# One run for attention, output projection and query projection, with the sample group's attention steps inside the projection's tiles

## The reference, cut to what matters

```
s    = q k^T * 64**-0.5 - slope_h * |i - j|       # two maps per head, 4 heads, blocks of 128 queries
attn = softmax(s[0]) - lam * softmax(s[1])
o_da = head_rms(attn @ v) * (1 - lam_init)
o_hg = head_rms(o_fwd + o_bwd) * silu(hg)         # o_fwd, o_bwd, silu(hg) come from earlier stages
x    = x + concat(o_hg, o_da) @ w_out
q    = rms_norm(x, g_ca) @ w_cq                   # queries of the cross attention that follows
```

## Time and profile before

| | |
|---|---|
| median of 3 runs | 2218.47 us (2218.03 to 2220.35) |
| the profiled execution, its own time | 2217.62 us |
| its span, first to last instruction | 2216.1 us |
| PE / DVE / ACT busy over the span | 89% / 61% / 53% |
| attention stage, first load to barrier | about 726.6 to 944.4 us |
| output projection | about 944.4 to 1108.7 us |
| query projection | about 1108.7 to 1234.6 us |

### The profile page before, as it was taken

One profiled execution on the slowest core, in us unless ns is written; L12 is line 12 of the kernel. 1 busy time (PEld: TensorE's weight loads), 2 busy tenths in 40 slices (PEclk: granted clock), 3 DMA queues, 4 the chain that ended last, 5 costly groups with the idle time before them and its releaser, 6 DMA issues. The chain is left out here.

```text
span 2216.1 us, 31313 instructions
## 1 busy us (share of the span) xinstructions
PE 1978.8 (89%) x11108; PEld 1640.8 (74%) x11108; DVE 1362.0 (61%) x1801; ACT 1180.8 (53%) x1767; POOL 265.2 (12%) x304
## 2 busy tenths in 40 slices
PE   6999999979999699559889499986999999999990
PEld 5888888858888376448778388875888888888870
DVE  4222231019997588646411035546999999999986
ACT  4334432118776588713222133222888888888873
POOL 0000000020000011100000000000122232332210
PEclk9999999989999799779989699996999999999995
DMA  5223422136552400244233423234999999999987
GB/s 171 97 93 135 151 98 105 46 105 188 177 174 91 176 15 15 74 147 169 77 120 115 138 90 111 72 148 148 337 384 379 383 379 383 375 379 391 385 315 318
DMA packets 162984, 423.98 MB, mean 191 GB/s; under 512 B 18880, under 2 KB 84544, under 8 KB 136768
## 3 DMA queue, kind: packets, MB, share of 16 engines
q1 hardware_dynamic: 137424, 342.37, 43.1%
q0 software_dynamic: 25456, 80.24, 9.4%
HBM read 354.92 MB, written 82.31 MB: 197 GB/s over the span
## 5 line engine op out<-in xcount | busy, mean ns | idle before, releaser
L113 PE MATMUL cross_ot_ps<-w_w_high,cross_o_high 128*128 128x512 f32 x544 | 220.7, 406 | 2.9 <-DVE cross_o_low L2140 2.4
L115 PE MATMUL cross_ot_ps<-w_w_high,cross_o_low 128*128 128x512 f32 x544 | 213.9, 393 | 0.0
L113 PE MATMUL front_acc<-in_high,front_w_high 128*128 128x512 f32 (+1 forms) x480 | 170.5, 355 | 0.0
L114 PE MATMUL front_acc<-in_low,front_w_high 128*128 128x512 f32 (+1 forms) x480 | 170.2, 354 | 0.0
L115 PE MATMUL front_acc<-in_high,front_w_low 128*128 128x512 f32 (+1 forms) x480 | 170.0, 354 | 0.0
L2107 DVE TENSOR_TENSOR cross_low_up<-cross_raw_up,w_w_high 128x2048 fp32r<-128x2048 f32 x68 | 152.8, 2289 | 12.1 <-ACT w_w_high L1918 12.1
L2107 DVE TENSOR_TENSOR cross_low_down<-cross_raw_down,w_w_low 128x2048 fp32r<-128x2048 f32 x68 | 152.7, 2287 | 1.7 <-ACT w_w_low L1918 1.6
L2107 DVE TENSOR_TENSOR w_w_low<-cross_raw_gate,w_w_high 128x2048 fp32r<-128x2048 f32 x68 | 152.2, 2279 | 0.0
L1918 ACT ACTIVATE w_w_high<-cross_raw_up 128x2048 fp32r<-128x2048 f32 x68 | 126.2, 1908 | 0.0
L1918 ACT ACTIVATE w_w_low<-cross_raw_down 128x2048 fp32r<-128x2048 f32 x68 | 126.1, 1906 | 0.0
L1918 ACT ACTIVATE w_w_high<-cross_raw_gate 128x2048 fp32r<-128x2048 f32 x68 | 126.0, 1902 | 0.0
(11 more groups left out here) (364 smaller groups left out, 4984.0 us busy)
## 6 DMA issues: line engine op xcount, KB each, us to landing
cross_raw_gate<-in_w_gate_dram SPq DMA_DIRECT2D x68, 1024.0 KB, 7.3
cross_raw_down<-in_w_down_dram SPq DMA_DIRECT2D x68, 1024.0 KB, 7.8
cross_raw_up<-in_w_up_dram SPq DMA_DIRECT2D x68, 1024.0 KB, 9.2
front_raw<-in_w_in_dram SPq DMA_DIRECT2D x32, 512.0 KB, 4.4
hgrn_raw<-in_w_ckv_dram SPq DMA_DIRECT2D x16, 512.0 KB, 6.4
cross_y_kept<-y_rows SPq DMA_DIRECT2D x16, 512.0 KB, 9.5
k_t<-front_staged POOLq DMA_DIRECT2D x8, 640.0 KB, 3.3
lf_t<-front_staged_lf POOLq DMA_DIRECT2D x8, 640.0 KB, 4.6
```

The costliest lines, as they stand in the source:

```text
L113: pe.matmul(out, lhs[0], rhs[0], start=first, stop=False)
L114: pe.matmul(out, lhs[0], rhs[1], start=False, stop=False)
L115: return pe.matmul(out, lhs[1], rhs[0], start=False, stop=last)
```

## The change

One function, `attend_mix_query`, takes the place of the three. There is one program block and so one barrier at its end. All orders are written out without loops.

Buffers of the later part are laid over those of the earlier part that are dead by then (query, keys and bias of the first three heads become `of`, `ob`, `silu`, `mixed` and the split of `mixed`; the normalised tokens go over the last head's bias, values, scores and probabilities). The eight PSUM banks are divided anew: `out_ps` has banks 0 and 1, the transposes of `mixed` one bank (2) instead of two, the sample scores banks 3 and 4, `xt_ps` banks 6 and 7; the query accumulators are banks 2 to 4 and 5 to 7.

The prompt's query, keys and values are loaded without the sample's tokens, which come in three loads of their own after them. The split of `w_out` moves from the last 8 steps to the prompt steps 2, 5, 8, ... 23. The first tiles' `sum_heads` and `gate` run in the prompt steps 25 to 30. The transposes of `mixed`, their split, the product and the residual are cut into halves of 512 columns with semaphores of their own. The 8 sample steps are cut up and placed at "points": point p = 2t + half is one half of tile t's product, and step s has its scores in the middle of product s + 2, transposes after product s + 3, output after product s + 4. The query projection starts right behind the last product. Its moving operand is `h_t`, which holds tokens in tiles (tile, high or low, k, 128), so that a 512-column operand is four runs of 128 columns.

```diff
-    steps = [(first, seq, h, t) for first, seq in ((0, SEQ_P), (SEQ_P, SEQ_S)) for h in range(HEADS) ...]
-    riders = {N - KC + r: r for r in range(KC)}
+    steps = [(h, t) for h in range(HEADS) for t in range(NT_P)]                 # N = 32
+    s_steps = [(h, t) for h in range(HEADS) for t in range(NT - NT_P)]          # NS = 8
+    riders = {2 + 3 * r: r for r in range(KC)}
+    first_point = 2
# GpSimd's queue
+                for t in range(NT):
+                    for p in (2 * t, 2 * t + 1):
+                        s = p - first_point - 2
+                        if 0 <= s < NS:
+                            store_sample(s)        # waits for s_o_done, s_head_norm(s)
+                    if t >= 1:
+                        store_x1(t - 1)
+                        if t + 1 < NT:
+                            load_x(t + 1)          # waits for the store of tile t - 1 to land
# VectorE
+                for n in range(-4, N):
+                    attention(n + 2); head_norm(n); find_least(n + 4)   # each where in range
+                    if n in riders: subtract_out(riders[n])
+                    if n == N - 7: sum_heads(0)
+                    if n == N - 6: gate(0)
+                    if n == N - 5: sum_heads(1)
+                    if n == N - 4: low_part(0, 0); gate(1)
+                    if n == N - 3: low_part(0, 1); sum_heads(2); low_part(1, 0); residual(0, 0)
+                    if n == N - 2: low_part(1, 1); gate(2); residual(0, 1)
+                for t in range(1, NT):
+                    sum_heads(t + 2); scale_next(t - 1); low_part(t + 1, 0); low_next(t - 2)
+                    for half in range(2):
+                        s = 2 * t + half - first_point
+                        s_find_least(s)
+                        residual(t, half)
+                        s_attention(s)
+                        if half == 0: low_part(t + 1, 1)
+                        s_head_norm(s - 2)
+                        if half == 0: gate(t + 2)
+                subtract_query(0); low_next(last_tile - 1); scale_next(last_tile); ...
# ScalarE, in a tile t
+                    find_next_rstd(t - 1); round_mixed(t + 1, 0); round_next(t - 2)
+                    for half in range(2):
+                        s_exps(s); s_copy_attention(s - 1); s_attention_rstd(s - 2)
+                        if half == 0: head_rstd(t + 2); round_mixed(t + 1, 1)
# TensorE
+                def s_transposes(s):
+                    pe.wait_ge(s_attn_done, s + 1)
+                    pe.wait_ge(s_attn_t_done, s)
+                    pe.wait_ge(s_score_read, min(s + 2, NS))
+                    ...
+                def product(t, half):                # waits m_low_done, x1_half_done or x1_done
+                    for k in range(KC):
+                        product3(...)
+                        if k == KC // 2 - 1: s_scores(s)
+                    s_transposes(s - 1); s_output(s - 2)
+                mixed_transposes(1, 0)               # after the scores, outputs, transposes of step N - 4
+                output(N - 2)
+                product(0, 0)
+                transposes(N - 1)
+                mixed_transposes(1, 1)
+                product(0, 1)
+                output(N - 1)
+                for t in range(1, NT):
+                    mixed_transposes(t + 1, 0); product(t, 0)
+                    mixed_transposes(t + 1, 1); product(t, 1)
+                    next_transposes(t - 1)
+                queries(0, 0)                        # waits q_low_done 1 and xt_low_done 4
+                next_transposes(last_tile)
+                queries(0, 1)
+                queries(0, 2)
+                for c in range(1, blocks):
+                    for group in range(3): queries(c, group)
# the caller
-            diff_attention(...); mix_out(...); project(...)
+            attend_mix_query(...)
```

More of the change, by code:

```diff
@@ L154, in rows_of @@
     return rows[ds(i * (2 * P) + u * P, P), :]
[L157 to L185, removed]
@@ L188, in project @@
[L188 to L297, removed]
@@ L1145, in _, with attend_mix_query @@
                 output(NT - 1, 1)
[L1148 removed]
+def attend_mix_query(nc, tag, dq_t, dk_t, dv_rows, g_da, lam, w_out, o_fwd, o_bwd, g_rows, mix, x_rows, g_hg, x1_out,
+                     g_next, w_cq, q_out, w_co, w_high, w_low, ident, eps):
     slopes = [2.0 ** (-8.0 * (h + 1) / HEADS) for h in range(HEADS)]
[L1154 to L1157, removed]
[L1158 to L1192 removed]
@@ new lines, in _ @@
+                load_heads(1)
+                load_attention(0)
+                load_attention(1)
+                for t in range(2, NT):
+                    load_heads(t)
+                    load_attention(t)
+                sp.wait_ge(mixed_done, NT)
+                load_query_weight(0)
+                load_query_weight(1)
+                sp.wait_ge(out_ready, 2 * NT)
+                load_co(0)
+                load_co(1)
+                for c in range(2, blocks):
+                    load_query_weight(c)
+                    load_co(c)
@@ new lines, in _ @@
+                for n in range(-4, N):
+                    if 0 <= n + 2 < N:
+                        attention(n + 2)
+                    if n >= 0:
+                        head_norm(n)
+                    if n + 4 < N:
+                        find_least(n + 4)
+                    if n in riders:
+                        subtract_out(riders[n])
+                    if n == N - 7:
+                        sum_heads(0)
+                    if n == N - 6:
+                        gate(0)
+                    if n == N - 5:
+                        sum_heads(1)
+                    if n == N - 4:
+                        low_part(0, 0)
+                        gate(1)
+                    if n == N - 3:
+                        low_part(0, 1)
+                        sum_heads(2)
+                        low_part(1, 0)
+                        residual(0, 0)
+                    if n == N - 2:
+                        low_part(1, 1)
+                        gate(2)
+                        residual(0, 1)
@@ L1269, in _ @@
+                subtract_query(0)
+                low_next(last_tile - 1)
+                scale_next(last_tile)
+                subtract_query(1)
+                low_next(last_tile)
+                for c in range(blocks):
+                    if c + 2 < blocks:
+                        subtract_query(c + 2)
+                    subtract_co(c)
             @block.scalar
@@ L1278, in exps @@
                 def exps(n):
[L1279 removed]
+                    u = n % 2
                     act.wait_ge(score_read, n + 1)
```

742 lines of the change are left out of this document (515 added, 227 removed).

## The result

The changed kernel takes **2193.85 us** (median of 4 runs, 2192.68 to 2196.01), the kernel before 2218.25 us beside it (2217.55 to 2220.35): ratio 0.989, 95% interval 0.9872 to 0.9907. That is 24.4 us faster. The forecast was 57.7 us, range 2146 to 2182: the sign is right, and more than half of the gain is missing; the time lies outside the range. The profiled execution is the one of 2192.68 us, span 2191.0; its mean granted clock is 0.953.

A forecast was written before the change was run, and what follows sets the result against it. PE was taken to bound products, query projection and prompt steps, with DVE and ACT nearly full in the latter; two seams held 95 us, PE needing 35.5. Terms summed to -57.7 us, giving 2160.8 us from a 2218.5 median, range 2146 to 2182.

The forecast's parts named there:

- The rows of `w_out`: Prompt steps: splitting eight `w_out` rows there costs ACT nothing and delays DVE 0.38 us each, +3.0 us, bounds 0 and 9.2.
- The block's end: Behind the query projection's last copy: nothing changes, since `q_t`'s store outlasts the last `w_co` row; 0 us.
- Ten tiles: Products with sample steps in them: 129.4 to 145.9 us, +16.5, bounds 139.4 and about 159.
- the loop of 18.3 us: Tiles 3 and 4: x arrives late through POOL's queue, 9.7 us plus 8.6 to the last head norm, setting the tile length.
- The first seam: Last prompt step's `find_least` to first product: 78.2 to 14.8 us, -63.4, as sample steps, barrier and fresh loads vanish.
- the second: Seam from last product to first query product: 17.0 to 1.9 us, -15.1, bounds 0.9 and 5.
- heads and gates: First tiles' `sum_heads` and `gate` in prompt steps: next `find_least` 1.4, then 2.1 us late, +3.5 us, bounds 0 and 4.4.
- The start: Before the first `find_least`: fewer tokens queued ahead of the small gain row, so DVE opens sooner, -2.7 us.
- rival (d): Query projection: split moving operands run at a lower rate, 1.1 us per cent, 2271 us at double; chance 0.04.
- (a): Tiles: PE alone sets them, x arrives in time and riders are free, 2147 us; chance 0.15.
- (b): Sample tiles: PE idles 2 to 4 us in tiles 3 to 5, falling to half clock each time, 2168 to 2184; chance 0.2.
- (c): Tiles: sample steps cost what they cost alone, some 4.5 us each, 36 in place of 16.5, 2180 us; chance 0.08.

The follow-up runs named there:

- e1: The changed kernel with DVE subtracting each row of `w_out` one step later in its queue: 2170.59 us.
- e7: The kernel of e1 with PE's first product placed ahead of the second tile's half transpose instead of behind it: 2169.09 us.
- e6: The kernel of e1 with GpSimd storing and loading x first in each tile turn, the two sample stores behind: 2165.27 us.
- e8: The changed kernel with the late subtraction, an added GpSimd drain after its last store of x, and x first in GpSimd's turn: 2160.07 us.
- e10: The kernel of e1 with an extra GpSimd drain behind 34 of its 68 DMAs, ahead of its loop over tiles: 2167.72 us.

## Why the prediction was wrong, and where it was right

**The rows of `w_out`: the failed step.** It was this sentence: ACT "is ahead of its consumer, so it costs nothing", and with it the +3.0 us, 0.38 a row, for DVE. The runs showed 27.9 us in its place, 3.5 a row. The work was sized nearly right: with the wait removed (e1) a row costs 0.42 to 0.45 us, although its 1.04 us of rounding don't fit into the 0.51 that ACT has spare in one step. What the sum left out is that DVE's subtraction needs ACT's rounding of the same step, and that ACT's place for it is at the end of a step that waits for PE's output. DVE reaches the subtraction 2.5 us before that. Moving a pair of operations on two engines adds an edge between their queues, and I priced the two operations and not the edge. It stood in a row that I had read: the subtraction in the earlier trace rows is preceded by 2.53 us of idle for that very rounding. I took its 1.23 us and dropped the bracket. Nor was that wait harmless where it stood. The view of that line, and PE's next transposes, in the kernel before:

```profile
  ACT w_w_high L179: 13.7, 8
913.97 0.44 PE L1333 MATMUL da_attn_ps<-kept_ident,da_prob 128*128 128x128 f32 x2 [2.58 <-DVE da_prob L1252]
```

All eight rows together held DVE for 13.7 us, the first one kept PE waiting 2.58 us behind it, and from one `find_least` to the next it took 5.63 us there (908.46 to 914.09) for 2.27 just before. The granted clock, 1.00 until then, fell about 1 us after that stop. So this very wait made the sample steps of before longer. The upper bound of 9.2 us (no slack at all) was too low because it bounded work only. Eight times the bracket, 8 x 2.53 = 20.2, would have been most of the missing term; the runs showed 24.3 us between the changed kernel and e1 in these steps (27.9 less 3.6), of which some 3 go with the two falls of the clock.

**The block's end: not seen.** "After the last copy nothing changes" looked at `q_t`'s store and the `w_co` row, which was true, and not at the barrier. One block in place of three collects 68 DMAs on GpSimd for one drain (5.6 us), where the query projection had 8 (0.7). The rows were in the trace of before, among the sequencers' instructions. The Trainium skill (VectorE: DVE Perf Modes, The DRAIN you can't avoid) describes, beside the pipeline flush, a boilerplate drain of about 12 ns on every engine, from a kernel's preamble and postamble. At the barrier SyncE's drain (7 ns) and ScalarE's (14 ns) are as short; those at this block's end are not, on any engine (0.12 us for SyncE, 1.26 for DVE, 5.61 for GpSimd).

**Ten tiles: the right size by luck.** 147.7 for 145.9 and 2 of clock. Tiles 1 to 5 lasted 14.8, 15.9, 16.3, 16.3 and 14.1 us for 14.6, 16.1, 18.3, 18.3 and 14.4. The late x is real, in tiles 3 to 6, but 1.9 to 3.5 us of it in tiles 3 to 5 are hidden from PE: the loop of 18.3 us doesn't exist. (Its 9.7 is also a wrong sum: the terms given add up to 9.4.) From x's store to the load's issue it takes 3.4 to 3.9 us there (983.17 to 986.63, 1015.77 to 1019.65), where I took 5.1. It bites once, in tile 6, where the load is issued 6.3 us after the store (1029.40) and takes 5.3 to land: PE stands 3.65 us, and the slower clock behind it makes tile 7 last 14.5 for 12.9. On the other side I sized a sample step at 1.3 us of PE and it is 1.69: with x in time the tiles are 142.6, not 139.4. The scores were too cheap in that sum (0.83 us for 0.55), and the small wait for `s_find_least` was not in it. The errors cancel nearly.

**Right as argued.** The first seam (15.3 for 14.8), with e7 for its mechanism, the second (2.1 for 1.9), and heads and gates in sum (3.5, 1.8 and 1.6 for 1.4 and 2.1). The start came out at 738.10 for 738, in part by luck: from the first load's issue to the first `find_least` 1.8 us were saved, not 2.7, and the stages ahead ended 1.1 sooner in this execution. The query copies are 13.77 us apart as before:

```profile
L1566 ACT ACTIVATE amq_staged<-amq_banks x8: 1237/1242/1242, 1100.4 to 1196.8; 128x1280 f32<-128x1280 f32 x8
```

(1196.8 - 1100.4) / 7 = 13.77, so moving operands in four runs of 128 columns cost nothing, and rival (d) is refuted. The Trainium skill's rule on SBUF cachelines, cited in the prediction, is not contradicted by it.

**The rivals.** (a), PE alone in the tiles, is right on the mechanism for all of them but tile 6 and the slow clock behind it, at another price. (b) is refuted: the clock falls once in the tiles, behind the one long stall, and in e6 it is 1.00 over all ten with the same matmuls going round the same banks. But the argument against (b), that PE would be busy enough to hold its clock, is no safe one: in the prompt steps of the changed kernel PE is busy 83%, and the clock falls behind two of the rows. The rule of the Trainium skill (TensorE: Matmul & The Clock Gate, A second HAM failure mode) that the prediction set beside (b) doesn't show here; nor did it in the sample stretch of before, where the clock fell once and stayed low for 58 us, without a swing. (c) is refuted: 1.69 us a step in place of 4.5.

The forecast of 2161 is what e8 measures (2160.07), which doesn't make it right: e8 has no late x and no 5 us at the end, and I had neither the 5 us nor the true price of a sample step.

## What to carry to other kernels

When work moves into a full pipeline, write down for each moved operation what it waits for and where that producer stands in its own queue at that moment, and read the idle time in front of the operation in the old trace as well as its duration: such a wait moves along with the operation, and in a full pipeline all of it becomes step length. Give a consumer on a second engine one step of distance from its producer; here one line bought 23 us. Before several blocks are fused, look at the drains and barriers at their ends: costs that go with a count are collected behind the last store.

## What the hardware showed unexpectedly

- GpSimd's drain lasts 0.082 us for every DMA that GpSimd has issued since its last drain (0.70, 1.36, 2.83, 3.58, 5.61, 7.26 us for 8, 16, 34, 43, 68, 88). An added drain in an idle stretch takes it off the end. That one can last longer than its count gives (8.56 us behind 60 DMAs, where it began with the issue of a store of x; 3.40 behind 34). Why, no run shows.
- Clearing 72 semaphores at a block's end in place of 12 takes 0.42 for 0.09 us.
- In the prompt steps of the changed kernel PE stood 1.26 and 1.54 us in each of the eight steps with a row, and the granted clock fell behind two of them only, 0.76 over 7 us; after the stop of 3.65 us in tile 6 it was 0.71 in the window shown. In each of these windows PE was thus partly at 1.2 GHz. Each of the three falls cost some 1.4 to 1.7 us (a step of 5.98 or 5.90 for 4.54 and 0.3 in the step after the latter, a tile of 14.54 for 12.93). A stop alone doesn't decide it: in e10 PE stood 3.72 us at the same place, the clock stayed at 1.00, and the next tile lasted 12.98.

```profile
1019.68:1023.08 3.40, 3.40 (x17) 2.86 (x18) 3.16 (x5) 2.63 (x6) 0.53 (x1) 1.00 0.68 270
```
